# Two transformer blocks with product-key experts on one core: unit 0's rows gathered in the query product, dense parts ahead of the row sums

## The reference

```
q = (h @ w_query).reshape(t, 8 heads, 2 halves, 128)
s1 = q[:, :, 0] . keys_1     s2 = q[:, :, 1] . keys_2        # 128 keys a half
v1, i1 = top_k(s1, 16)       v2, i2 = top_k(s2, 16)
cand = v1[..., :, None] + v2[..., None, :]                     # 256 a head
top_s, pos = top_k(cand, 16);  idx = i1 * 128 + i2 at pos
gate = softmax(top_s)
act = gelu(expert_down[idx] . h);   out = sum(gate * act * expert_up[idx])
```

## Time and profile before

| | us |
|---|---|
| median of 3 runs | 4063.46 (4062.32 to 4066.45) |
| the profiled execution: its own time | 4071.76 |
| its span | 4070.0 |
| TensorE busy | 3364.2 (83%) |
| VectorE busy | 2390.2 (59%) |
| GpSimd busy | 1642.3 (40%) |
| ScalarE busy | 819.2 (20%) |

### The profile page before, as it was taken

One profiled execution on the slowest core, in us unless ns is written; L12 is line 12 of the kernel. 1 busy time (PEld: TensorE's weight loads), 2 busy tenths in 40 slices (PEclk: granted clock), 3 DMA queues, 4 the chain that ended last, 5 costly groups with the idle time before them and its releaser, 6 DMA issues.

```text
span 4070.0 us, 41343 instructions
## 1 busy us (share of the span) xinstructions
PE 3364.2 (83%) x14084; PEld 1717.2 (42%) x14084; DVE 2390.2 (59%) x4282; ACT 819.2 (20%) x1934; POOL 1642.3 (40%) x1133
## 2 busy tenths in 40 slices
PE   8998998999988786456888899989888865568888
PEld 6343434444865453111222267457655531112222
DVE  3787885410287778876455422422877788765553
ACT  1222224300111013663000002220111137630000
POOL 0000000000066566677566500000566666887664
PEclk9999999999999898667898899979999986679899
DMA  6343432344389999889999963422899988999998
GB/s 212 111 125 101 123 116 95 103 144 145 121 314 374 370 376 353 298 333 362 341 400 386 363 209 100 143 83 106 323 366 376 372 329 291 339 323 368 377 361 332
DMA packets 316846, 1064.60 MB, mean 262 GB/s; under 512 B 95666, under 2 KB 104770, under 8 KB 216002
## 3 DMA queue, kind: packets, MB, share of 16 engines
q0 software_dynamic: 147456, 717.84, 46.6%
q1 hardware_dynamic: 134240, 335.05, 23.3%
q10 hardware_dynamic: 34960, 9.27, 1.0%
HBM read 1415.93 MB, written 2.10 MB: 348 GB/s over the span
## 4 chain that ended last, share of the span: by engine, by line
PE 48%; DMA 20%; DVE 13%; issue 9%; POOL 5%; ACT 3%; SPq 1%; ACTq 0%; DVEq 0%; POOLq 0%; another core or an unknown queue 0%
PE bank L701 12%; DMA big<-in_peer_down,sc 8%; DMA big<-in_peer_u,sc 7%; PE bank L1057 5%; PE bank L1116 5%; POOL big L635 5%; PE bank L1040 4%; PE bank L759 4%; PE bank L715 4%; DMA wring<-in_dense_up 4%; PE bank L996 4%; DVE sc L2129 3%; PE bank L866 2%; PE bank L1175 1%; ACT wring L1528 1%
## 5 line engine op out<-in xcount | busy, mean ns | idle before, releaser
L2129 DVE CUSTOM_DVE_ANT_0 sc<-big,hs 128x2048 f32<-128x2048 f32 x512 | 1174.1, 2293 | 644.8 <-DMA big<-in_peer_down,sc 328.2
L1116 PE MATMUL bank<-big,sc 128*32 128x512 f32 x4096 | 653.6, 724 | 103.1 <-DVE sc L2148 56.8
L1057 PE MATMUL bank<-wring 128*128 128x512 f32 x1024 | 540.9, 665 | 88.2 <-DMA wring<-in_dense_up 82.6
L701 PE MATMUL bank<-wring,ht 128*128 128x512 f32 x1280 | 582.2, 612 | 0.8 <-DVE ht L1939 0.8
L635 POOL DMA_INDIRECT big<-in_peer_up,sc x256 | 412.0, 1609 | 302.5 <-PE bank L1116 169.4
L1040 PE MATMUL bank<-ht,wring 128*128 128x256 f32 x2048 | 519.9, 407 | 0.9 <-ACT wring L1503 0.9
L635 POOL DMA_INDIRECT big<-in_peer_v,sc x256 | 399.7, 1561 | 277.3 <-PE bank L1116 154.3
L1040 PEld LDWEIGHTS bank<-ht,wring 128*128 128x128 f32 x2048 | 398.9, 202 | 211.8 <-issue 157.2
L635 POOL DMA_INDIRECT big<-in_peer_u,sc x256 | 413.2, 1614 | 179.9 <-DVE sc L2103 81.0
L635 POOL DMA_INDIRECT big<-in_peer_down,sc x256 | 391.1, 1528 | 189.2 <-DVE sc L2103 81.1
L1057 PEld LDWEIGHTS bank<-wring 128*128 128x128 f32 x1024 | 194.0, 205 | 440.2 <-issue 315.9
(11 more groups left out here) (388 smaller groups left out, 3297.1 us busy)
## 6 DMA issues: line engine op xcount, KB each, us to landing
wring<-in_w_in SPq DMA_DIRECT2D x84, 1024.0 KB, 5.3
wring<-in_dense_down SPq DMA_DIRECT2D x64, 1024.0 KB, 8.9
wring<-in_dense_up SPq DMA_DIRECT2D x256, 256.0 KB, 7.8
wring<-in_w_out SPq DMA_DIRECT2D x32, 1024.0 KB, 5.0
wring<-in_w_attn_o SPq DMA_DIRECT2D x16, 1024.0 KB, 5.0
wring<-in_peer_w_query SPq DMA_DIRECT2D x16, 1024.0 KB, 4.8
wring<-in_peer_w_q SPq DMA_DIRECT2D x16, 1024.0 KB, 4.8
wring<-in_glu_w_a SPq DMA_DIRECT2D x8, 1024.0 KB, 5.0
```

What stands on the lines that cost most here:

```text
L701: mm = pe.matmul(dense_bank[2 * pair + t][:, 0:w_cols], lhs[:, k, t * P:(t + 1) * P], wslot[:, b, kk * w_cols:(kk + 1) * w_cols], start=(k ...
L1057: mm = pe.matmul(dense_out[t][:, :], dense_w[:, r, t * P:(t + 1) * P], sup[:, m % 2, r % 4, :], start=(r == 0), stop=(r == DENSE - 1))
L1116: mm = pe.matmul(acc_bank[j][32 * q:32 * q + 32, :], w_blocks[:, u % 2, g, :], gslot[:, m % RING, q * 512:(q + 1) * 512], start=(u % PH == ...
L2129: v.tensor_tensor_reduce(dot_out, gslot[:, m % RING, :], h[:, u // PH, :], 1.0, 0.0, ALU.mult, ALU.add, sub(rAC)[:, i:i + 1]).then_inc(dot ...
```

## The change

1. The query chunks come in the order head 0 first half, head 0 second half, first halves of heads 1 to 7, second halves of heads 1 to 7, with four weight slots (0 to 3) instead of six. The works between parts move by a chunk: second square sums to chunk 9, turn and list to chunk 10, turned indices to chunks 12 and 14.
2. The first-half keys lie in `wring` slot 7 and the squares in slot 6, which the product no longer uses, so no gather waits for the scores. TensorE waits for all four key tiles ahead of the first scores.
3. VectorE decodes unit 0's rows (`decode_rows`) as soon as head 0's scores are there and releases its gathers with indices that are not masked; eleven of its dots come ahead of the second squares, the twelfth ahead of the list, four after unit 1's decode. The masks and gates (`decode_gates`) come after the list. The weights of masked rows are zero as before.
4. Decode treats both halves in one instruction of 512 columns each, instead of two of 256.
5. In each step TensorE makes down quarters and up parts first, then the row sum.
6. At the start the squares come ahead of the gain copy, and row scale 1 between tile 0's pieces.

```diff
-QUERY_SLOTS = (0, 1, 2, 3, 6, 7)
-MORE_USES = (1, 1, 1, 1, -2, -2, 0, 0)
+QUERY_SLOTS = (0, 1, 2, 3)
+MORE_USES = (2, 2, 2, 2, -2, -2, -2, -2)
...
+QUERY_ORDER = [(0, 0), (1, 0)] + [(half, hd) for half in range(2) for hd in range(1, PH)]
+EARLY_DOTS = 11
...
-        keyT = [w.rearrange("p (j c) -> p j c", j=PH) for w in (big[:, 14336:15360], sub(rBL))]
+        keyT = [w.rearrange("p (j c) -> p j c", j=PH) for w in (wring[:, 14336:15360], sub(rBL))]
...
-        squares = dot_out.rearrange("p (t h c) -> p t h c", t=NT, h=PH)
+        squares = wring[:, 12288:14336].rearrange("p (t h c) -> p t h c", t=NT, h=PH)
...
                 if m == 6:
                     pool.wait_ge(keys_evac, 4 * (layer + 1))
-                elif m == 7:
-                    pool.wait_ge(sk_evac, CHUNKS * layer + PH)
...
-                pe.wait_ge(keys_evac, 4 * layer + i // 4 + 1)
+                pe.wait_ge(keys_evac, 4 * layer + 4)
...
-                    elif (i, part) == (8, 2):
+                    elif (i, part) == (9, 2):
                         sum_squares(layer, 1)
-                    elif (i, part) == (9, 1):
+                    elif (i, part) == (10, 1):
                         turn_sums(layer)
-                    elif (i, part) == (9, 3):
+                    elif (i, part) == (10, 3):
                         list_product(layer)
-                    elif i in (11, 13) and part == 2:
-                        turn_early(layer * UNITS + i // 2 - 5)
+                    elif i in (12, 14) and part == 2:
+                        turn_early(layer * UNITS + i // 2 - 6)
...
-                        if u:
-                            row_sums(layer, u - 1, g)
                         for i in range(quarter_at(n), quarter_at(n + 1)):
                             down_quarter(layer, i)
                         for i in range(up_part_at(n), up_part_at(n + 1)):
                             up_part(layer, i)
+                        if u:
+                            row_sums(layer, u - 1, g)
...
-                    if i in (9, 10):
-                        peer_soft(layer * UNITS + i - 9, i - 9)
+                    if i in (3, 13):
+                        peer_soft(layer * UNITS + i // 8, i // 8)
...
+            v.wait_ge(x_loaded[0], 16)
+            squares_of(0, 0, D).then_inc(squares_ready, 1)
             v.wait_ge(gain_turned, 1)
             st.link(v.tensor_copy(gain_cols, mb[0][:, 0:64]))
-            v.wait_ge(x_loaded[0], 16)
-            squares_of(0, 0, D).then_inc(squares_ready, 1)
             row_scales(0, 0)
-            take_tile(0, 0)
+            take_tile(0, 0, (0, 1))
             row_scales(0, 1)
+            take_tile(0, 0, (2, 3))
             take_tile(0, 1)
...
-                for s in range(2):
-                    hot = sub((rW2, rCB)[s]).rearrange("p (a b) -> p a b", a=TOPK)
...
+                hot = sc[:, rW2[0]:rCA[1]].rearrange("p (a b) -> p a b", a=2 * TOPK)
+                st.link(v.tensor_tensor(hot, sub(rPF).unsqueeze(2).broadcast_to([P, 2 * TOPK, 16]),
+                                        iota16.unsqueeze(1).broadcast_to([P, 2 * TOPK, 16]), ALU.is_equal))
...
+                st.link(v.tensor_reduce(tok_sel[:, t, 0:2, cols], hot, AX, ALU.add))
...
+                if u == 0:
+                    v.tensor_copy(d_idx[:, mine], sub(rIX)).then_inc(stage_ready, 1)
...
-                choose_keys(layer, 0, 0)
+                for s in range(2):
+                    choose_keys(layer, 0, s)
+                choose_pairs(0)
+                decode_rows(base, 0)
                 square_scores(layer, 0)
+                for k in range(EARLY_DOTS):
+                    row_dot(layer, 0, k)
                 square_scores(layer, 1)
                 rank_keys(layer)
-                choose_keys(layer, 0, 1)
+                row_dot(layer, 0, EARLY_DOTS)
                 list_keys(layer)
-                choose_pairs(0)
-                decode(base, 0)
+                decode_gates(base, 0)
                 for s in range(2):
                     choose_keys(layer, 1, s)
                 collect(base, 0)
                 choose_pairs(1)
                 decode(base + 1, 1)
+                for k in range(EARLY_DOTS + 1, TOPK):
+                    row_dot(layer, 0, k)
```

More of the change, by code:

```diff
@@ L77, in query_slot @@
 def query_slot(i, r_pq):
-    b = QUERY_SLOTS[i % 6]
-    return b, uses(b, r_pq) + i // 6
+    b = QUERY_SLOTS[i % 4]
+    return b, uses(b, r_pq) + i // 4
+QUERY_ORDER = [(0, 0), (1, 0)] + [(half, hd) for half in range(2) for hd in range(1, PH)]
+EARLY_DOTS = 11
 class Steps:
@@ L502, in query_weights @@
                     sp.wait_ge(wused[b], r)
-                    sp.dma_start(wslot[:, b, :], w[i]).then_inc(wfull[b], 16)
+                    half, hd = QUERY_ORDER[i]
+                    sp.dma_start(wslot[:, b, :], w[half * PH + hd]).then_inc(wfull[b], 16)
             query_weights(R_PQ, a["peer_w_query"])
@@ L958, in key_scores @@
                     mm = pe.matmul(mb[i % 2][:, t * P:(t + 1) * P], pqT[:, i % 3, t * P:(t + 1) * P],
-                                   keyT[i // PH][:, i % PH, :], start=True, stop=True)
+                                   keyT[half][:, hd, :], start=True, stop=True)
                 mm.then_inc(sk_done, 1)
@@ L1502, in peer_head @@
                     act.wait_ge(sk_done, CHUNKS * layer + i + 1)
-                    act.activation(score_of[:, :, i % PH, i // PH, :],
+                    half, hd = QUERY_ORDER[i]
+                    act.activation(score_of[:, :, hd, half, :],
                                    mb[i % 2][:, 0:T].rearrange("p (t c) -> p t c", t=NT), ACT.Copy).then_inc(sk_evac, 1)
-                    if i in (9, 10):
-                        peer_soft(layer * UNITS + i - 9, i - 9)
+                    if i in (3, 13):
+                        peer_soft(layer * UNITS + i // 8, i // 8)
             def dense_gelu(layer, p):
@@ L1728, in row_scales, with take_tile @@
                 v.tensor_scalar(h[:, t, 0:P], ident, stat[:, 6 + t:7 + t], None, ALU.mult).then_inc(diag_ready, 1)
-            def take_tile(m, t):
-                for kk in range(4):
+            def take_tile(m, t, which=range(4)):
+                for kk in which:
                     n, col = batches[0], 16 * m + 4 * kk
@@ L2024, in choose_keys @@
                 if u < PH:
-                    v.wait_ge(sk_evac, CHUNKS * layer + PH * s + u + 1)
+                    v.wait_ge(sk_evac, CHUNKS * layer + QUERY_ORDER.index((s, u)) + 1)
                 st.link(v.max(val[:, c:c + 8], src))
@@ L2034, in square_scores @@
                 some = slice(4 * part, 4 * part + 4)
-                v.wait_ge(sk_evac, CHUNKS * layer + 4 * part + 4)
+                v.wait_ge(sk_evac, CHUNKS * layer + QUERY_ORDER.index((0, 4 * part + 3)) + 1)
                 for t in range(NT):
@@ L2076, in choose_pairs, with decode_rows @@
                 st.link(v.max_index(pos[:, 8:16], top[:, 8:16], sub(rCB)))
-            def decode(unit, u):
+            def decode_rows(unit, u):
                 b, t, hd = u % 2, u // PH, u % PH
@@ L2102, in decode @@
                 st.link(v.scalar_tensor_tensor(sub(rIM), sub(rFL), float(SKIP), sub(rIX), ALU.mult, ALU.add))
-                v.tensor_copy(d_idx[:, mine], sub(rIM)).then_inc(stage_ready, 1)
+                if u:
+                    v.tensor_copy(d_idx[:, mine], sub(rIM)).then_inc(stage_ready, 1)
                 v.tensor_tensor(sub(rCA)[:, 0:P].rearrange("p (i k) -> p i k", i=TOK_G),
@@ L2114, in decode @@
                 st.link(v.tensor_tensor(gate_m[:, mine], sub(rFL), gate, ALU.mult))
+            def decode(unit, u):
+                decode_rows(unit, u)
+                decode_gates(unit, u)
             def collect(unit, u):
@@ L2221, in peer_units @@
                         n = u * TOPK + k
-                        if u < UNITS:
+                        if 0 < u < UNITS:
                             row_dot(layer, u, k)
```

20 lines of the change are left out of this document (11 added, 9 removed).

## The result

The changed kernel is slower: 4081.8 us (median of 20 runs, 4067.4 to 4095.0) against 4067.7 (20 runs of the kernel before on the same chip, 4049.6 to 4078.5), ratio 1.0032 with a 95% interval of 1.0020 to 1.0043. That is 13 us more, between 8 and 18. 15 us less were forecast.

The account below looks back on a forecast made before the run. It took a TensorE-bound query product with idle transfers, then a loop mostly transfer-bound, and chain-bound just after decodes. Start -3.7, query product -16.6 and steps +5 gave -15.3 us: 4056.5 profiled, 4048.2 plain median, range 4036 to 4062.

Parts of the forecast that it names:

- The steps: Expert steps, dense parts ahead of row sums: 11.5 us a block less 8.0 for decodes, taken as +2.5 a block, +5.
- much of the lateness disappears in a full queue: Gathers behind late row sums: queueing hides part of the delay, so +3.5 us a block was taken as +2.5.
- the upper bound: The steps' worst case, every microsecond lost at the borders: 10 x 4.6 - 8 = +38 us a block.
- Rival D: At 20 borders the row sum waits behind two slow quarters, the ring runs dry, 3.0 us each: +24, 4087 us; chance 0.15.
- Query product: Query product: unit 0's early gathers bring row sums forward, 8.3 us a block gained, -16.6 us for two.
- rival C: Query product: gathers don't fit beside query weights at 366 GB/s, TensorE waits 9.6 us: -4.3, 4059 us; chance 0.15.
- Decode: Decode of rows in 512-column instructions: 0.57 us less each, 14 decodes a block, 8.0 us a block.
- Start: Kernel start: squares before the gain copy, first projection at 17.5 instead of 21.39 us: -3.7 us.
- Dense up parts: Steps with dense up parts: they alternate alike and only shift by one sum: nothing, between -3 and +3 us.
- Weight blocks: Row sums waiting for weight blocks: dense parts fill the 1.8 us wait, leaving 0.5 us lateness at five borders a block.
- Rival B: Steps: the order costs nothing, as TensorE fills waits and gathers queue anyway: -44, 4019 us; chance 0.20.
- rival E: Query product: early rows bring nothing, as unit 1's later indices set the pace: 4065 us; chance 0.05.

Follow-up runs that it names:

- after: The changed kernel with all six parts of the change, against the kernel before: 4081.8 us, ratio 1.0032.
- rows_first: The changed kernel with the row sum ahead of the dense parts again in every step: 4035.0 us, ratio 0.9927 to the kernel before.
- order_only: The kernel before with one edit, dense parts ahead of the row sum in each step: 4118.2 us, ratio 1.0122.
- row_before_turn: The quickest kernel: the changed one, dense part first only in each half unit's first step, elsewhere row sum ahead of turned indices and quarters: 4017.2 us, ratio 0.9874.
- query_only: The kernel before with the query product's part of the change alone, old step order, decode and start: 4056.5 us, ratio 0.9983.
- two_quarters_rows_first: The changed kernel with the row sum first only in steps that make two quarters: 4049.1 us, ratio 0.9958.
- border_rows_first: The changed kernel with the row sum first only in the 14 steps a block that turn indices: 4062.5 us, ratio 0.9990.

## Why the prediction was wrong

Its sign failed at one step, **The steps**. It priced the new order at 11.5 us a block (5 x 1.8 + 5 x 0.5); measured, it is 21 in after (10.5 thousandths for two blocks) and 25 on the kernel before. That term was mis-sized, in both of its kinds. Between the starts of one turned indices and the next, after is longer than rows_first by 2.7 us in the half units that begin at a border without a turn of the weights (ten in both blocks), where 1.8 was forecast, and by 1.4 us in those that begin at a border with one (eight), where 0.5 was forecast; order_only against the kernel before gives 2.9 and 1.1. These are single traces, but the two pairs agree. Two things led to the sizes.

- It said that "the gather that leads to the next decode hangs on the third sum, a step with one quarter: 1.8 us", and priced that one gather. But GpSimd issues in order and every slot with up rows hangs on its own sum: the border steps cost 17 us in the 20 that have quarters, 0.9 each, which alone is less than the forecast's 23, and the two steps behind it cost 20 more. The 11.5 held nothing for them beyond that third sum. How the lateness of these two sums passes on to the next decode was not traced.
- It took 1.0 us a block off, since "much of the lateness disappears in a full queue". It did not: the share fell to 0.51 for four us at the border shown, and up to the tenth turned indices the traces of after and rows_first differ by 23.6 us in block one and 14.5 in block two.

A smaller one, which entered only the upper bound: the slot of the border's sum was to come free 4.6 us later. It is 5.5 (6.34 and 1.07 in after, for 1.94 in the earlier trace rows), as the quarters now take the slow stretch that the sum took before.

With 43 to 50 us instead of 23 for the order, no discount, and every other term of the sum as it stood, the forecast would have been about +7 to +14; 13 was measured. That this reaches 13 at its upper end is in part luck, since the other terms were forecast at 36 us together and are worth 30 in rows_first: 43 less 30 is 13.

Rival D had the sign, and got a chance of 0.15. It had the row sum behind two quarters, the low clock and the dry ring, and all of these are in the rows above, but it laid 3.0 us on the sum of each of 20 borders. The borders themselves cost 0.9 each, below the 1.8 from which D said it decides; only with the two steps behind, which D does not name, is it 1.9, and 2.1 to 2.5 with all steps. So D was right in sign and in part in place, and its size was too large. A hint at more than 1.8 us was in the earlier trace rows: waits of up to 7.1 us lie ahead of the sum, and two quarters were to be put behind them. Neither the forecast nor D asked what it costs that sum and wait stand in this order, which was so in the kernel before, too: 14 us (row_before_turn).

The other terms:

- **Query product**, -16.6: the mechanism is right in each place. First gather at 1058.7 (about 1061 was forecast), wait ahead of the second square sums 1.7 us (2.7), the transfers at 407 GB/s over 50 us beside the query weights (400 taken), so rival C is out. The lead at the first row sum is 6.5 us relative to the product's start (7.7). The time is 7 us for two blocks in the run with this part alone, with 12 at most, so 16.6 was too much. Which step of it failed stays open: in the trace of that run the product up to the first turned indices is 5.7 and 9.2 us shorter (171.0 and 167.8 for 176.7 and 177.0), together close to the forecast, and the span still shows it; but the trace of the kernel before is a long one, and no timed run separates the lead from what is lost behind it.
- **Decode**, -16.0 in the sum (28 decodes): 14 measured, for 32. Right within the interval (9 to 18).
- **Start**, -3.7: right at the first projection, 0 at the end.
- The three alone add to 21 us, and rows_first, which has all three, to 30. Each of these has an interval of 4 to 7 us to either side; whether they help each other stays open.
- **Dense up parts**, nothing between -3 and +3: 2, right. **Weight blocks**: the wait was filled as forecast (56.8 to 16.9 us), and leading with the dense part there gave some 8 us, if the overlap of intervals is set aside; of the places tested it is the only one where the new order may pay.
- Rival B (order free) is refuted by rows_first and order_only, rival E by query_only, whose interval lies below 1, if only just (0.9996).

Of the order's 43 us in after, the borders and the two steps behind account for 37 and the late steps for 2; 4 are within what these measurements can tell. What stays open is how much of the 20 us belongs to which of the two steps behind; two_quarters_rows_first suggests the one with two quarters.

## What to carry to other kernels

When one engine frees the slots of a ring that another engine refills in program order, put the instruction that frees a slot ahead of everything that it does not depend on, filler work and waits alike. Here filler work in front of the row sums cost 43 us, nearly all of it at and just behind the places where TensorE had waited; and 28 row sums moved in front of such a place (20 of them with a wait there) gave 14 us. Filler work may lead where the freeing instruction itself waits (here the first step of a half unit); where the queue runs without a stall, as in the steps of the dense up parts, the order cost nothing that could be measured. To price a delay at a stall, do not follow one gather only: the steps behind the stall cost as much as the stall itself. Nor does the longest pause between two freed slots give the price, as the pause of 6.7 us in border_rows_first and of 13.4 in the quickest kernel show.

## What the runs showed of the hardware

The two quarters behind a border took 6.34 us, in the open 3.72 (both rows above, of 16 matmuls each). TensorE had been idle for 6.8 us, and its granted clock in the stretch 1236 to 1240 is 0.50, the 1.2 GHz level; from 1241 to 1242 it is 0.52, and from 1242 on 1.00, 2.4 GHz. All but the last microsecond of these quarters was thus at half speed, 2.6 us more. The order decides which work pays: in the earlier trace rows the row sum took 1.94 us and the quarters 5.47; in open steps they take 1.07 and 3.72.

The pair of query weights and gathers ran at 424 GB/s over ten us with TensorE in its product. The section that the prediction drew on, the Trainium skill ("DMA: Bandwidth & Descriptors", Where 436 GB/s comes from), lets the HBM side bind such transfers at about 358 for a core, but also calls a measured 425 GB/s near the rate of the fabric. The trace agrees with the second figure; the first did not bind here, nor in the stretch of the earlier trace rows, so the -2 us that the prediction worked out from it do not apply.
